# A running merge of three attention groups, wide value matmuls for the new tokens, and other staging buffers in a decoder layer on eight cores

## The chip, the cores and the metric

The kernel runs on all 8 cores of one Trainium2 chip. Each core takes one prompt of 2048 tokens and 4 of the 32 sample tokens (one new token each), and holds all weights for itself; the cores exchange nothing. The time of a run is that of the slowest core, in microseconds (us). Each core has TensorE (PE, matmuls; its weight loads are shown as PEld), VectorE (DVE), ScalarE (ACT), GpSimd (POOL) and SyncE (SP, which here only issues DMAs). Matmuls write to PSUM, which is addressed here as banks of 512 f32 per partition; everything else lies in SBUF or, for long distances, in DRAM scratch.

## What is computed

One decoder layer for the prompt and for the sample tokens. The part that the change touches is the dilated attention: 12 heads of 128 in 3 groups g of 4 heads h, with dilations 1, 4 and 16. A query of a group sees 128 keys of its own residue class modulo the dilation.

```python
for g in range(ATT_GROUPS):                       # 3 groups, 4 heads each
    o, lse, kb, vb = attention(aq[:, :, g], ak[:, :, g], av[:, :, g], dil=(1, 4, 16)[g], 128 keys, bias)
    outs.append(o); lses.append(lse)              # o = P V / den,  lse = max + log(den)
alpha = softmax(stack(lses), axis=0)              # weights of the groups
att_out = sum(alpha * stack(outs), axis=0)        # (tokens, 4 heads * 128)
mixed = sigmoid(gr) * (ret_out @ w_rb) + sigmoid(ga) * (att_out @ w_ab)
x = x + mixed @ w_o
x = x + square(relu(rms_norm(x) @ w_u)) @ w_d
x = x + sigmoid(x @ w_pg) * (ple @ w_pl)
```

Beside it run a retention branch (chunks of 128 tokens, 8 heads), whose output is `ret_out`, and the caches: keys and values of the last 128, 512 and 2048 positions of each group are outputs. For a sample token, the 128 rows of a cache that its query sees, with the new row in place of one, are gathered by stride; scores, softmax over all three groups and values follow.

## The kernel before

**Order of the work.** The Python code records every instruction (an `Op`) with what it reads and writes. `schedule()` (L278) is a planner: a list scheduler with a cost for each instruction, priority by order of recording, and for a DMA a cost of issue (0.55 us on SP) and a latency after its bytes (`DMA_LATENCY`, 2.2 us). `emit()` writes out each engine's instructions in the order that it found, and they wait for each other by semaphores (L397). On the chip this order is fixed: when an instruction waits, everything behind it on its engine waits.

**Stages**, by the times of the profiled execution: norm and transpose of x (0 to 84 us), attention groups 0 and 1 (to about 360 us), group 2 with the values of the sample tokens and the first retention chunks (to 500 us), the other retention chunks (to 733 us), gates and output projection (mix), MLP, and the per-layer embedding at the end (1133 to 1538 us).

**Projections.** L680 is the matmul of `gemm()`: 8 matmuls of 128x512 accumulate one block of a projection. Keys and values of a group are computed with tokens on partitions (`tm_pair`, `tm_full`), copied from PSUM by DVE into one of 5 staging buffers `kvst` (L840), and stored from there to the cache outputs by a DMA (kp, vp); a staging buffer is free again when its store has landed. L847 transposes keys.

**A block of attention.** `scores()`: L903 the matmul, L916 scale and bias (DVE), L919 the negated maximum of each row into `md` (DVE), L922 the exponential with its sum (ACT). `values()`: L933 transposes of P (PE), L937 their copy (DVE), L944 P times V (PE). `core(g, h)` runs 16 tiles of a head, in 4 blocks of 4 tiles, for the groups 0 and 1: L969 copies the unnormalised output from PSUM to `ogs` (DVE), SP stores it to the DRAM scratch `oscr`; negated maxima and denominators go to the scratch `mscr`.

**The merge** is in `core_last(h)`, the third group. For each head the maxima and denominators of groups 0 and 1 are loaded (`ml`), and for each block the outputs of both (`ogl`, 512 KB, in 4 buffers, two of which are named ogx). L1009 to L1021 find the common maximum, the exponentials `ee` of the differences, the denominator and the normalised weights. POOL multiplies the output of group 0 (L1049) and of group 1 in every second block (L1054); ACT does the latter in the other blocks (L1060); POOL adds both (L1063). `finish()` (L1027) takes the product and sum with group 2's own PSUM result, 4 DVE instructions of 128 columns a block; L1035 transposes it (PE), L1038 copies it to `attT` (ACT).

**Sample tokens.** `sample_values(b)` loads, for token b, the 128 value rows of three groups (256 KB each) into `smk` and `smq`, and behind each the one new row into the same buffer. Its inner `rest()` records L1141: for each of 4 heads and 3 groups one f32 matmul with the values as weights and one column of probabilities, 12 in all; L1145 copies the 4 columns. The loads of token h are recorded at head h of group 2, the matmuls at head h+1, the last ones within retention chunk 1.

**Other names.** wr are the 6 weight blocks of the retention (`load_wr`, POOL's queue). `ret_open`, `ret_proj`, `ret_in`, `ret_mix`, `ret_norm` and `ret_sample` are the steps of a retention chunk (L1253 to L1518). `d2d(n)` issues n copies of cache rows, DRAM to DRAM. `ple_in(t)` (L1804) loads a tile of the per-layer embedding through a ring of 4 buffers `pp` and transposes it. L714 is a small f32 matmul for the bias tables at the start.

## Time and profile before

| | us |
|---|---|
| runs, median (three: 1540.83, 1551.37, 1553.70) | 1551.37 |
| profiled execution, its own time | 1539.19 |
| its span, first to last instruction of the slowest core (core 1) | 1538.1 |
| spans of the 8 cores | 1511.6 to 1538.1 |
| mean granted TensorE clock of the 8 cores | 0.965 to 0.971 |

The profile is one execution, on its slowest core. "Busy" is time in which an engine executes; it waits in the rest. The idle time of a group of instructions is what its engine waited just before them, with the engine or DMA that ended the wait. The granted clock is TensorE's: 1.00 is 2.4 GHz, its lower level is 1.2 GHz (0.50). The DMA share is the mean over the core's 16 DMA engines.

### The profile page before, as it was taken

How to read it: one execution, taken by the hardware profiler on the slowest of the kernel's cores; microseconds unless marked ns; L12 is line 12 of the kernel's file. 1: busy time of each engine (PE TensorE's matmuls, PEld its weight loads, DVE VectorE, ACT ScalarE, POOL GpSimd, SP SyncE). 2: the span in 40 equal slices, each digit the busy share in tenths (PEclk: the TensorE clock that was granted, in tenths of full speed). 3: DMA queues.
4: the chain of work that ended last, by engine and by line, in shares of the span. 5: the costliest groups of instructions: out<-in, count | busy, mean ns of one | idle time of the engine just before them, and what ended most of it. 6: DMA issues, size and time to landing. Idle time of an engine off the chain costs nothing.

```text
span 1538.1 us, 25714 instructions; the slowest of 8 cores (1511.6 to 1538.1 us)
## 1 busy us (share of the span) xinstructions
PE 1433.7 (93%) x8657; PEld 771.1 (50%) x8657; DVE 864.5 (56%) x1651; ACT 621.7 (40%) x1354; POOL 259.2 (17%) x287
## 2 busy tenths in 40 slices
PE   4799999897776999997999999999999998999997
PEld 2565555464453445554555554554454444554443
DVE  2654656564554466664434346546656645557776
ACT  2455555444553557675222225431121120220665
POOL 2400000000453454454100001100000000000111
PEclk9899999998886999998999999999999999999999
DMA  9695716788783411108812044799999999730112
GB/s 227 117 153 99 141 53 104 143 199 173 152 200 64 87 39 36 36 26 166 121 28 29 4 89 129 126 140 163 179 157 160 173 161 152 156 69 14 60 79 83
DMA packets 123233, 172.44 MB, mean 112 GB/s; under 512 B 28990, under 2 KB 94583, under 8 KB 122336
## 3 DMA queue, kind: packets, MB, share of 16 engines
q0 software_dynamic: 55200, 43.52, 22.6%
q1 hardware_dynamic: 66368, 83.28, 20.6%
q10 hardware_dynamic: 1536, 43.99, 14.5%
q8 instruction: 72, 1.18, 0.3%
q14 instruction: 57, 0.47, 0.1%
HBM read 184.95 MB, written 75.68 MB: 169 GB/s over the span
## 4 chain that ended last, share of the span: by engine, by line
PE 84%; DMA 6%; issue 3%; ACT 2%; DVE 2%; POOL 1%; SPq 0%; another core or an unknown queue 0%; DVEq 0%; ACTq 0%; POOLq 0%
PE psum L680 74%; PE psum L801 2%; DMA vp<-kvst 1%; DMA kp<-kvst 1%; PE psum L1141 1%; DMA wi<-w_in 1%; PE psum L903 1%; PE psum L933 1%; PE psum L944 1%; DMA xt<-x 1%; ACT pr L922 1%; DMA smq<-vs 1%; PE psum L1447 1%; PE psum L1509 1%; DMA mscr<-md 0%
## 5 line engine op out<-in xcount | busy, mean ns | idle before, releaser
L680 PE MATMUL psum<-wm,rT 128*128 128x512 bf16 (+1 forms) x1088 | 240.1, 379 | 0.0
L680 PE MATMUL psum<-h2T,wm 128*128 128x411 bf16 (+1 forms) x1280 | 227.0, 340 | 0.0
L1801 DVE TENSOR_TENSOR xb<-psum,xb 128x512 f32<-128x512 f32 (+1 forms) x272 | 187.5, 690 | 42.4 <-PE psum L680 31.0
L680 PE MATMUL psum<-wr,hT 128*128 128x512 bf16 x768 | 187.2, 395 | 7.7 <-ACT gs L1300 3.1
L680 PEld LDWEIGHTS psum<-h2T,wm 128*128 128x128 bf16 x1280 | 124.8, 98 | 99.4 <-issue 3.3
L1787 DVE TENSOR_TENSOR rT<-psum,rl 128x411 bf16<-128x411 f32 (+1 forms) x160 | 93.6, 586 | 143.5 <-ACT rl L1785 143.4
L680 PEld LDWEIGHTS psum<-wm,rT 128*128 128x128 bf16 (+1 forms) x1088 | 104.6, 97 | 128.4 <-issue 4.1
L680 PE MATMUL psum<-hT,wi 128*128 128x512 bf16 x640 | 152.5, 384 | 6.5 <-DMA wi<-w_in 3.3
L1785 ACT ACTIVATE rl<-psum 128x411 f32<-128x411 f32 (+1 forms) x160 | 82.1, 513 | 142.5 <-PE psum L680 142.4
L680 PE MATMUL psum<-hT,t1w 128*128 128x411 bf16 (+1 forms) x640 | 120.5, 341 | 4.6 <-ACT sg L1658 4.6
L680 PE MATMUL psum<-wi,hT 128*128 128x512 bf16 (+1 forms) x496 | 118.1, 386 | 3.5 <-DVE kvst L840 3.5
L680 PEld LDWEIGHTS psum<-wr,hT 128*128 128x128 bf16 x768 | 74.0, 101 | 93.0 <-issue 21.8
L922 ACT ACTIVATE pr<-sc,md 128x128 bf16<-128x128 f32 (+1 forms) x192 | 88.6, 461 | 28.3 <-DVE md L919 17.4
L680 PEld LDWEIGHTS psum<-hT,wi 128*128 128x128 bf16 x640 | 61.4, 99 | 69.4 <-issue 11.1
L680 PEld LDWEIGHTS psum<-hT,t1w 128*128 128x128 bf16 x640 | 62.7, 98 | 54.8 <-issue 7.0
L680 PEld LDWEIGHTS psum<-wi,hT 128*128 128x128 bf16 (+1 forms) x496 | 59.0, 126 | 43.8 <-issue 8.0
L1660 DVE TENSOR_TENSOR mm<-psum,sg 128x411 f32<-128x411 f32 (+1 forms) x40 | 23.3, 585 | 99.0 <-PE psum L680 98.9
L1816 ACT COPY pT<-psum 128x256 bf16<-128x256 bf16 (+1 forms) x17 | 5.5, 364 | 181.2 <-PE psum L1812 181.2
L919 DVE TENSOR_REDUCE md<-sc 128x2 f32<-128x512 f32 (+3 forms) x100 | 54.8, 549 | 28.6 <-ACT pr L922 26.6
L1656 ACT ACTIVATE sg<-psum 128x411 f32<-128x411 f32 (+1 forms) x40 | 20.5, 513 | 113.3 <-PE psum L680 86.6
L916 DVE SCALAR_TENSOR_TENSOR sc<-psum,bias 128x512 f32<-128x512 f32 (+2 forms) x100 | 53.2, 549 | 22.9 <-PE psum L903 21.9
L680 PE MATMUL psum<-wm,x2T 128*128 128x512 bf16 (+1 forms) x272 | 61.5, 379 | 0.8 <-ACT x2T L1866 0.8
(202 smaller groups left out, 1973.1 us busy)
## 6 DMA issues: line engine op xcount, KB each, us to landing
ks<-ck ACTq DMA_DIRECT2D x16, 1023.5 KB, 28.1
vs<-cv ACTq DMA_DIRECT2D x16, 1023.5 KB, 24.7
oscr<-ogs SPq DMA_DIRECT2D x32, 256.0 KB, 4.6
wm<-w_up POOLq DMA_DIRECT2D x8, 1024.0 KB, 35.5
wm<-w_dn POOLq DMA_DIRECT2D x8, 1024.0 KB, 49.9
y<-xb SPq DMA_DIRECT2D x16, 512.0 KB, 2.6
kt<-rk SPq DMA_DIRECT2D x17, 432.0 KB, 3.3
xr<-x SPq DMA_DIRECT2D x14, 512.0 KB, 3.9
```

The lines of the kernel that those rows point to most:

```text
L680: ins = e.matmul(out, lhsT=l, rhs=r, start=(i == 0), stop=(i == n - 1))
L801: ins = e.matmul(ps[:, bi, 256 * i:256 * (i + 1)], lhsT=stream_ap(hT[:, k, :], 1, t + i), rhs=wv[:, k, 256 * hp:256 * (hp + 1)], start=(k ...
L903: i = e.matmul(ps[:, sb_, c:c + nk], lhsT=qT[:, 128 * t:128 * (t + 1)], rhs=kT[:, k0:k0 + nk], start=True, stop=True)
L916: dve.op(lambda e, c=c, n=n, nk=nk, sv=sv, bv=bv: e.scalar_tensor_tensor(out=sv, in0=ps[:, sb_, c:c + n * nk].rearrange("p (i k) -> p i k" ...
L919: dve.op(lambda e, i=i, n=n, sv=sv: e.tensor_reduce(out=md[:, 0, i:i + n], in_=sv, axis=AX.X, op=ALU.max, negate=True), reads=[sc_t], writ ...
L922: act.op(lambda e, i=i, c=c, nk=nk: e.activation(out=pr[:, c:c + nk], in_=sc[:, c:c + nk], func=AF.Exp, bias=md[:, 0, i:i + 1], accum_out= ...
L933: i = e.transpose(out=bankbf(pi)[:, c:c + 128], in_=pr[:, c:c + 128], identity=identb)
L1656: act.op(lambda e, s1=s1, b=b, w=w: e.activation(out=s1[:, 0:w], in_=ps[:, b[0], 0:w], func=AF.Sigmoid), reads=[bank_t[b[0]]], writes=[s1_t])
L1660: dve.op(lambda e, s1=s1, m1=m1, b=b, w=w: e.tensor_tensor(out=m1[:, 0:w], in0=ps[:, b[2], 0:w], in1=s1[:, 0:w], op=ALU.mult), reads=[bank ...
L1785: act.op(lambda e, rl=rl, b=b, w=w: e.activation(out=rl[:, 0:w], in_=ps[:, b, 0:w], func=AF.Relu), reads=[bank_t[b]], writes=[rl_t])
L1787: dve.op(lambda e, rl=rl, b=b, w=w, r=r, fi=fi, ts=ts: e.tensor_tensor(out=r[:, fi, ts], in0=ps[:, b, 0:w], in1=rl[:, 0:w], op=ALU.mult), ...
L1801: dve.op(lambda e, b=b, xv=xv, rows=rows: e.tensor_tensor(out=xv, in0=ps[0:rows, b, :], in1=xv, op=ALU.add), reads=[bank_t[b], x1_t[t]], w ...
```

## The change

1. *The merge runs along.* In group 1, each head loads group 0's maxima and denominators, and each block group 0's output (`oga`, a ring of 2). `scores()` takes the smaller of its own negated maximum and that of before (new L929, DVE), so that both are relative to one maximum. A block takes the difference (L998, DVE), its exponential (L1000, ACT), scales the loaded output by it (L1002, POOL) and adds it to its own result in place of the copy (L1006, DVE); at the end of a head the denominators are added (L1017, L1018). Group 2 does the same with the output of group 1 alone, which holds both by now, and multiplies by the reciprocal of the denominator on POOL at the end (L1050), ahead of the transposes (now L1058).

```diff
+    def scores(g, h, ts, Bt, B_t, md, md_t, before=None):
...
+        if before is not None:
+            nm, nm_t = before
+            dve.op(lambda e: e.tensor_tensor(out=md[:, 0, :], in0=md[:, 0, :], in1=nm, op=ALU.min), reads=[md_t, nm_t], writes=[md_t])
...
+            dd, ee = cw[:, 0:16], cw[:, 16:32]
...
+            if g == 1:
+                oa, oa_t, oakey = state["oga"].next()
+                sp.dma(oa.rearrange("p (i c) -> p i c", i=4), oscr[0, h].rearrange("(i p r) c -> r p i c", p=128, r=4)[blk],
+                       oakey, reads=oscr_t[0][h], writes=[oa_t])
...
+                before = None
+                if g == 1:
+                    before = strm(ml[:, 0, :], blk)[:, i:i + 2], ml_t
+                u = scores(g, h, [t, t + 1], Bt, B_t, mdt(t), md_t, before)
...
+                dve.op(lambda e, blk=blk: e.tensor_tensor(out=strm(dd, blk), in0=strm(md[:, 0, :], blk), in1=strm(ml[:, 0, :], blk),
+                                                          op=ALU.subtract), reads=[md_t, ml_t], writes=[cw_t])
+                act.op(lambda e, blk=blk: e.activation(out=strm(ee, blk), in_=strm(dd, blk), func=AF.Exp), reads=[cw_t], writes=[cw_t])
+                a0, a0_t, _ = accring.next()
+                pool.op(lambda e, a0=a0, oa=oa, blk=blk: e.tensor_tensor(
+                    out=a0.rearrange("p (i c) -> p i c", i=4), in0=oa.rearrange("p (i c) -> p i c", i=4),
+                    in1=strm(ee, blk).unsqueeze(2).broadcast_to([128, 4, 128]), op=ALU.mult),
+                    reads=[oa_t, cw_t], writes=[a0_t])
+                dve.op(lambda e, og3=og3, ob=ob, a0=a0: e.tensor_tensor(out=og3, in0=bank(ob), in1=a0, op=ALU.add),
+                       reads=[bank_t[ob], a0_t], writes=[og_t])
...
+            dve.op(lambda e: e.tensor_tensor(out=ee, in0=ee, in1=ml[:, 1, :], op=ALU.mult), reads=[ml_t, cw_t], writes=[cw_t])
+            dve.op(lambda e: e.tensor_tensor(out=md[:, 1, :], in0=md[:, 1, :], in1=ee, op=ALU.add), reads=[md_t, cw_t], writes=[md_t])
```

In `core_last`, the weights of three groups give way to one `ee` and `den`:

```diff
+        dve.op(lambda e: e.tensor_tensor(out=dd, in0=md[:, 0, :], in1=ml[:, 0, :], op=ALU.subtract), reads=[md_t, ml_t], writes=[cw_t])
...
+        dve.op(lambda e: e.tensor_tensor(out=den, in0=ee, in1=ml[:, 1, :], op=ALU.mult), reads=[ml_t, cw_t], writes=[cw_t])
+        dve.op(lambda e: e.tensor_tensor(out=den, in0=den, in1=md[:, 1, :], op=ALU.add), reads=[md_t, cw_t], writes=[cw_t])
...
-                dve.op(lambda e, i=i: e.scalar_tensor_tensor(
-                    out=ak[:, 128 * i:128 * (i + 1)], in0=ps[:, ob, 128 * i:128 * (i + 1)],
-                    scalar=ee[:, 2, 4 * blk + i:4 * blk + i + 1], in1=a0[:, 128 * i:128 * (i + 1)],
-                    op0=ALU.mult, op1=ALU.add), reads=[bank_t[ob], cw_t, a0_t], writes=[ak_t])
+            dve.op(lambda e: e.tensor_tensor(out=a0, in0=bank(ob), in1=a0, op=ALU.add), reads=[bank_t[ob], a0_t], writes=[a0_t])
+            pool.op(lambda e: e.tensor_tensor(
+                out=ak.rearrange("p (i c) -> p i c", i=4), in0=a0.rearrange("p (i c) -> p i c", i=4),
+                in1=den[:, 4 * blk:4 * blk + 4].unsqueeze(2).broadcast_to([128, 4, 128]), op=ALU.mult),
+                reads=[a0_t, cw_t], writes=[ak_t])
```

2. *Values of the sample tokens.* The probabilities of 4 heads are now the weights and the rows of values stream, 512 columns at once; of the result, 4 rows of one bank at partition 32b, the row of head h is wanted only in the columns of head h. ACT copies it to `sov`, and after the fourth token `sample_out()` transposes all and picks the columns. The loads of token 0 are recorded right after the sample softmax; the loads of token h and the matmuls of token h-1 now follow the retention projections of head h, and the last matmuls are in chunk 1 as before. `ret_sample()` moves from chunk 1 to chunk 2.

```diff
+                for g in range(3):
+                    c = 16 * g + 4 * b
+                    ins = e.matmul(ps[32 * b:32 * b + 4, bi, :], lhsT=pT_s[:, c:c + 4], rhs=vts[g][0], start=(g == 0), stop=(g == 2))
                 return ins
...
+            act.op(lambda e: e.copy(out=state["sov"][32 * b:32 * b + 4, :], in_=ps[32 * b:32 * b + 4, bi, :]),
+                   reads=[bank_t[bi]], writes=[state["sov_t"]])
...
+        def tr(e):
+            for h in range(4):
+                ins = e.transpose(out=ps[:, bi, 128 * h:128 * (h + 1)], in_=state["sov"][:, 128 * h:128 * (h + 1)], identity=identf)
+            return ins
...
+        for h in range(4):
+            dve.op(lambda e, h=h: e.tensor_copy(out=attT[:, h, 2048:2052], in_=ps[:, bi, 129 * h:129 * h + 97:32]),
...
-        else:
-            later()
-        later = sample_values(h)
+            later = sample_values(0)
...
+            load_wr(5, marks[2, 0])
             load_wr(4, marks[2, 0])
...
-    load_wr(5, marks[2, 2])
+        if h:
+            later([])
+            later = sample_values(h)
```

3. *Planner.* The latency of a DMA becomes 3.2 us, its issue 0.7 us on SP, and `slack` adds 2.0 us to a load of sample rows and 6.0 us to the one-row load behind it.

```diff
-DMA_LATENCY = 2.2
+DMA_LATENCY = 3.2
...
-                    o.t1 = now + DMA_LATENCY
+                    o.t1 = now + DMA_LATENCY + o.slack
...
+        sp.dma(v, cache[b, 0:W:DILS[g], :], key, writes=t, after=state["x_in"], slack=2.0)
+        sp.dma(v[0:1, :], new[b, W - 1:W, :], key, reads=[new_t], writes=t, slack=6.0)
```

4. *Buffers.* `kvst` has 6 in place of 5, `sc` 3 in place of 4, `md` 4 in place of 2; `ogl` becomes four of 512 columns, and the `acc` ring gets the two `oga` buffers in group 2. The lower part of the region shrinks, and the last `load_wr` moves ahead, since its space is free earlier.

```diff
-        state["kv"], o = ringbuf("kvst", o, 512, F32, 5)
-        state["ac1"], o = ringbuf("ac1", o, 512, F32, 2)
+        state["kv"], o = ringbuf("kvst", o, 512, F32, 6)
+        state["oga"], o = ringbuf("oga", o, 512, F32, 2)
...
+            items.extend(ringbuf("ogx%d_" % i, OQ + 8192 * i + 4096, 512, F32, 2)[0].items)
+        accring.items.extend(state["oga"].items)
+        state["ogl"] = Ring(items[::2] + items[1::2])
```

5. *Later stages.* Five steps of the mix stage issue two `d2d` copies each. `ple_load(t)` is split from `ple_in(t)`, and `ple_in` runs one MLP step later.

```diff
+        if 1 <= f <= 5:
+            d2d(2)
...
+        if 2 <= j <= 7:
+            for t in range(3 * (j - 2), min(3 * (j - 1), 17)):
+                ple_in(t)
         if 1 <= j <= 6:
             for t in range(3 * (j - 1), min(3 * j, 17)):
-                ple_in(t)
+                ple_load(t)
```

**In the order of the instructions.** The first excerpt is from PE, at the last blocks of group 1's last head: L903 scores, L933 transposes of P (`pr`), L944 P times V (`vf`, `pT`), L847 transposes of keys. Before:

```order
L903 MATMUL psum<-qk_98 128x128
L903 MATMUL psum<-qk_98 128x256
L933 MATMUL psum<-identb,pr_77 128x128 x3
L944 MATMUL psum<-vf_100,pT_83 128x128 x3
L933 MATMUL psum<-identb,pr_78 128x128 x4
L944 MATMUL psum<-vf_100,pT_84 128x128 x4
L933 MATMUL psum<-identb,pr_79 128x128 x3
L944 MATMUL psum<-vf_100,pT_85 128x128 x3
L933 MATMUL psum<-identb,pr_80 128x128 x4
L944 MATMUL psum<-vf_100,pT_83 128x128 x4
L847 MATMUL psum<-identb,kb_112 128x128 x4
L847 MATMUL psum<-identb,kb_113 128x128 x4
```

Now, with L682 a projection (one row for 8 matmuls), L942 the transposes of P and L953 P times V:

```order
L682 MATMUL psum<-wi_51,hT 128x512 x8
L942 MATMUL psum<-identb,pr_76 128x128 x3
L682 MATMUL psum<-wi_50,hT 128x512 x8
L953 MATMUL psum<-vf_101,pT_82 128x128 x3
L682 MATMUL psum<-wi_51,hT 128x512 x8
L942 MATMUL psum<-identb,pr_77 128x128 x4
L953 MATMUL psum<-vf_101,pT_83 128x128 x4
L682 MATMUL psum<-wi_51,hT 128x512 x8
L942 MATMUL psum<-identb,pr_78 128x128 x3
L953 MATMUL psum<-vf_101,pT_84 128x128 x3
L942 MATMUL psum<-identb,pr_79 128x128 x4
L953 MATMUL psum<-vf_101,pT_82 128x128 x4
```

Four projections of the next group now stand in and around these four pairs of transposes and values (a fifth pair begins with the row above these); the last two pairs have none in them.

The second excerpt is also from PE, in group 2, where the matmuls for the values of a sample token (now L1155) stand. Before, the third token's 12 (L1141, the first of them is the last row here) came behind this:

```order
L944 MATMUL psum<-vf_101,pT_85 128x128 x4
L933 MATMUL psum<-identb,pr_79 128x128 x4
L680 MATMUL psum<-wr_124,hT 128x512 x8
L903 MATMUL psum<-kT_99,qk_98 128x128 x4
L680 MATMUL psum<-wr_125,hT 128x512 x8
L1035 MATMUL psum<-identb,atk_119 128x128 x4
L944 MATMUL psum<-vf_101,pT_83 128x128 x4
L944 MATMUL psum<-vf_101,pT_84 128x128 x4
L933 MATMUL psum<-identb,pr_80 128x128 x4
L1035 MATMUL psum<-identb,atk_120 128x128 x4
L903 MATMUL psum<-kT_99,qk_98 128x128 x8
L1141 MATMUL psum<-sm,smk_115 128x1
```

Now the rows from the second token's matmuls on are these (L1058 transposes of the merged block, L1340 and L1446 of the retention):

```order
L1155 MATMUL psum<-smk_118,sm 4x512
L1058 MATMUL psum<-identb,atk_120 128x128 x4
L942 MATMUL psum<-identb,pr_80 128x128 x4
L682 MATMUL psum<-wr_138,hT 128x512 x8
L1058 MATMUL psum<-identb,atk_121 128x128 x4
L953 MATMUL psum<-vf_102,pT_83 128x128 x4
L1340 MATMUL psum<-identb,qkr_135 128x128 x8
L942 MATMUL psum<-identb,pr_81 128x128 x4
L682 MATMUL psum<-wr_140,hT 128x512 x8
```

and on to the third token's:

```order
L953 MATMUL psum<-vf_102,pT_84 128x128 x4
L942 MATMUL psum<-identb,pr_76 128x128 x4
L682 MATMUL psum<-wr_140,hT 128x512 x8
L942 MATMUL psum<-identb,pr_77 128x128 x4
L1446 MATMUL psum<-qkT_128 128x128 x8
L953 MATMUL psum<-vf_102,pT_82 128x128 x4
L682 MATMUL psum<-wr_127,hT 128x512 x8
L1058 MATMUL psum<-identb,atk_119 128x128 x4
L953 MATMUL psum<-vf_102,pT_83 128x128 x4
L1155 MATMUL psum<-smk_116,sm 4x512
L1155 MATMUL psum<-smk_117,sm 4x512
```

Between the two there are four projections and thirteen shorter pieces; between the first and the second token's, not shown, there are seven and thirteen.

The third excerpt is from DVE, in group 1, near the end of the last head. Before, the output of a block is copied (L969) between scores (L916, L919) and the copy of P (L937):

```order
L969 COPY ogs_103<-psum 128x512
L1091 TENSOR_REDUCE sm<-smq_114 128x4
L919 TENSOR_REDUCE md_86<-sc_74 128x2
L1093 SCALAR_TENSOR_TENSOR sm<-sm 128x16
L916 SCALAR_TENSOR_TENSOR sc_75<-psum,bias_71 128x128
L937 COPY pT_84<-psum 128x384
L919 TENSOR_REDUCE md_86<-sc_75 128x1
L916 SCALAR_TENSOR_TENSOR sc_75<-psum,bias_71 128x256
```

Now the sum L1006 stands there, with `acc` from POOL, and the minima L929 and the difference L998 around it (L922 scale and bias, L925 the maximum, L946 the copy of P):

```order
L1006 TENSOR_TENSOR ogs_103<-psum,acc_94 128x512
L925 TENSOR_REDUCE md_87<-sc_73 128x2
L922 SCALAR_TENSOR_TENSOR sc_75<-psum,bias_71 128x512
L946 COPY pT_84<-psum 128x384
L929 TENSOR_TENSOR md_87<-md_87,ml_89 128x2
L998 TENSOR_TENSOR cw_92<-md_87,ml_89 128x4
L925 TENSOR_REDUCE md_87<-sc_74 128x1
L922 SCALAR_TENSOR_TENSOR sc_74<-psum,bias_71 128x256
L925 TENSOR_REDUCE md_87<-sc_74 128x1
L929 TENSOR_TENSOR md_87<-md_87,ml_89 128x2
L946 COPY pT_82<-psum 128x512
```

The sum has the next scores and the next copy of P behind it, and three small instructions have come in.

## Rows read from the trace of the kernel before

**Rows 1.** Busy time, share and instructions of each engine, from the page.

```profile
PE 1433.7 (93%) x8657; PEld 771.1 (50%) x8657; DVE 864.5 (56%) x1651; ACT 621.7 (40%) x1354; POOL 259.2 (17%) x287
```

**Rows 2.** Stretches: us, busy (count) of PE, PEld, DVE, ACT, POOL; PEclk, DMA share, GB/s.

```profile
84.00:269.00 185.00, 184.85 (x1238) 108.81 (x1236) 104.99 (x209) 101.51 (x276) 3.54 (x4) 1.00 0.60 110
269.00:345.00 76.00, 69.70 (x404) 41.26 (x404) 47.29 (x99) 33.84 (x88) 0.00 (x0) 0.98 0.80 168
345.00:400.00 55.00, 40.55 (x250) 22.92 (x250) 24.47 (x52) 32.37 (x109) 7.78 (x9) 0.88 0.91 174
400.00:450.00 50.00, 42.02 (x281) 28.92 (x281) 31.22 (x85) 23.85 (x81) 30.16 (x27) 0.81 0.67 157
450.00:500.00 50.00, 34.41 (x219) 20.11 (x217) 25.27 (x86) 22.95 (x51) 19.43 (x17) 0.67 0.44 110
```

**Rows 3.** The same view, of shorter stretches.

```profile
350.00:360.00 10.00, 6.08 (x33) 3.51 (x34) 4.20 (x8) 4.66 (x12) 0.00 (x0) 0.52 0.63 184
398.00:408.00 10.00, 9.54 (x42) 7.21 (x43) 0.72 (x3) 1.61 (x6) 3.20 (x3) 0.53 0.34 93
442.00:452.00 10.00, 8.94 (x40) 7.10 (x41) 3.50 (x11) 2.33 (x9) 5.35 (x5) 0.51 0.62 126
...
473.00:490.00 17.00, 9.96 (x44) 4.69 (x44) 7.91 (x23) 5.85 (x12) 11.54 (x11) 0.52 0.41 63
```

**Rows 4.** PE's groups, 200:500: instruction, count, busy, mean ns, idle before, releasers.

```profile
L680 PE MATMUL psum<-wi,hT 128*128 128x512 bf16 x288 | 70.2, 390 | 3.5 <-DVE kvst L840 3.5
...
L1141 PE MATMUL psum<-sm,smk 128*128 128x1 f32 x64 | 13.4, 313 | 12.0 <-ACT pr L922 6.0 <-DMA smq<-vs 5.6 <-ACT attT L1038 0.4
...
L1035 PE MATMUL psum<-identb,atk 128*128 128x128 bf16 x64 | 7.2, 243 | 6.2 <-DVE atk L1027 4.5 <-ACT attT L1038 1.6 <-ACT cw L1014 0.2
```

**Rows 5.** Chain that ended last, two stretches: start us, us, what.

```profile
266.27 18.00 DMA kp<-kvst
...
398.46 5.25 PE psum L1141 x24
...
409.98 1.73 PE psum L680 x8
...
422.12 2.72 PE psum L1141 x24
...
425.30 6.82 DMA smk<-cv
...
433.44 9.28 DMA smq<-vs
...
443.06 5.25 PE psum L1141 x24
...
491.67 4.23 PE psum L1141 x24
```

**Rows 6.** Timeline of PE near the start: start, us, instruction, what released it.

```profile
7.57 1.43 PE L714 MATMUL psum<-ohg,rbx 33*4 33x383 f32 x2 [7.57 <-DMA ohg<-ohg]
```

**Rows 7.** DMA issues: queue, count, KB each, median us from issue to landing.

```profile
ogl<-oscr SPq DMA_DIRECT2D x8, 512.0 KB, 7.2
...
pp<-pp POOLq DMA_DIRECT2D x16, 64.0 KB, 56.9
```

**Rows 8.** Groups by form, as in 4, of DVE (200:500) and POOL (200:510).

```profile
L1027 DVE SCALAR_TENSOR_TENSOR atk<-psum,cw,acc 128x128 bf16<-128x128 f32 x64 | 20.5, 346 | 3.0 <-POOL acc L1063 0.6 <-DVE atk L1027 0.2
...
L969 DVE COPY ogs<-psum 128x512 f32<-128x512 f32 x18 | 12.4, 691 | 9.0 <-PE psum L944 4.0 <-PE psum L903 2.9 <-PE psum L977 1.6
...
L1011 DVE TENSOR_TENSOR cw<-cw,ml 128x32 f32<-128x32 f32 x4 | 1.8, 458 | 0.2
...
L1015 DVE TENSOR_TENSOR cw<-cw,ml 128x32 f32<-128x32 f32 x4 | 0.8, 188 | 0.7 <-ACT cw L1014 0.7
...
L1063 POOL TENSOR_TENSOR acc<-acc,ac 128x512 f32<-128x512 f32 x16 | 20.0, 1265 | 2.3 <-ACT ac L1060 2.1
L1049 POOL TENSOR_TENSOR acc<-ogx,cw 128x512 f32<-128x512 f32 x8 | 8.3, 1040 | 7.3 <-DVE atk L1027 6.8 <-DVE cw L1018 0.4
```

163 lines of the change are left out of this document (74 added, 89 removed).

## The prediction

> **What bounds the kernel now.** I read the page's table of engines first: TensorE (PE) is busy 93% of the span [rows 1]. Then the stretches [rows 2]: from 84 to 269 us PE is busy 184.85 of 185 us, so nothing done there on another engine can gain. From 269 to 500 us it is busy 69.70, 40.55, 42.02 and 34.41 of 76, 55, 50 and 50 us: 6.3 + 14.4 + 8.0 + 15.6 = 44.3 us idle. This is the end of attention group 1, all of group 2, and the new tokens' values, and it is where the change works. No engine is full there: VectorE (DVE) has 25.27 of the last 50 us. So the loss is latency between engines in a fixed order, not throughput.
>
> The idle time has a second price. In four stretches of this region the granted clock is 0.51 to 0.53, the lower level (1.2 GHz), each behind or among waits of PE [rows 3]. PE is busy 6.08 + 9.54 + 8.94 + 9.96 = 34.5 us in them; at 2.4 GHz about half of it would do, 17 us less. The pool to win from is thus 44 + 17 us, 4% of the time.
>
> Who makes PE wait: values of the new tokens (L1141) 12.0 us, the transposes of the merged output (L1035) 6.2 us, projections behind a staging copy (L680 wi,hT, released by kvst L840) 3.5 us [rows 4]. The rest are gaps of about 1 us where the order holds nothing but links of one chain.
>
> **The change, part by part.**
> *Waits ahead of the sample values.* A bulk load lands, then a one-row load into the same buffer is issued; that 2 KB row took 9.28 us from issue to landing, although it is tiny [rows 5]. The planner had counted 2.2 us, and now counts 3.2 plus 6.0 for such a row. The chain of loads, 425.3 to 442.7 us in the trace, is 17 us. In the new order PE has seven projections and thirteen short pieces between the first and second group of value matmuls, and four and thirteen between the second and third (second excerpt of the order). At 1.73 us a projection [rows 5] and about 0.25 us a piece that is 15.5 and 10 us. So the first, second and last group should find their rows there within 2 us, and the third may lack up to 7, of which waits for the merge in between use some: 12.0 becomes 5. **-7** (bounds -12 and 0).
>
> *The matmuls themselves.* 48 with one column each, f32, took 5.25, 2.72, 5.25 and 4.23 us, 17.45 together [rows 5]; the 2.72 is at full clock. They become 12 with 512 columns, plus four f32 transposes. The trace has no such shape. Nearest is the f32 matmul of 383 columns (L714): 1.43 us for its two records [rows 6]. For 512 columns that is 1.91 us, or 0.96 if that row ran at the lower level, which it does not show. Twelve cost 11.5 or 22.9 us; L714 ran just after PE's first wait, as those stretches of half clock do, so I lean to the lower price and take 13.5. **-4** (bounds -6 and +6). A gain only by clock: at full level the old 48 would be 4 x 2.72 = 10.9 us.
>
> *Tail of group 1.* Of the 14.4 us idle in 345:400, 6 belong to the value wait at 398 us; the other 8 are the alternation of L933, L944 and L847 that the first excerpt of the order shows, about nine gaps. Afterwards four projections stand inside it, and two of the five pairs are still bare. **-3** (bounds -6 and 0).
>
> *Staging buffers 5 to 6.* The waits are DMAs of 256 KB that take up to 18.00 us to land [rows 5]; one more buffer gives one more copy of cover, but not more bandwidth. **-2** (bounds -3.5 and 0).
>
> *Merge in group 2.* Per head, DVE loses 16 instructions of 346 ns (L1027) for 4 of 512 columns, about 691 ns as L969 [rows 8]: 22.1 us less 11.1 over four heads. Of the small instructions nine leave and eight come: nothing. GpSimd (POOL) per block loses an add of 1265 ns and half a product of 1040 and gains one product [rows 8], ScalarE its 32 scalings. Against it, the merged block now passes through one more engine before its transpose: after the DVE sum a POOL product of 1.04 us and a hop. Per block 4 x 0.346 = 1.4 us on DVE become 0.69 + 1.04 + about 0.15. The path is half a microsecond longer, but the planner knows it and puts other work between; DVE, which everything else waits for, is freed by 11 us of the 81 it is busy from 345 to 500 us [rows 2]. The load of the sixth retention weight also moves ahead, since its space is free earlier. Of 15.6 us idle in 450:500 I take **-5** (bounds -10 and +6).
>
> *Merge in group 1.* New: 32 minima and 16 differences on DVE, near 0.18 us each (L1015), 8.6 us; 16 POOL products, 16 tiny exponentials, 16 loads of 256 KB, 8 of 8 KB. The DVE copy L969 becomes a sum of the same width. DVE is busy 47.29 of 76 us, so 8.6 us over 140 fit under PE. What can cost: the sum waits for POOL, POOL for the load; the third excerpt shows that behind it on DVE stand the next scores and the copy of P, for which PE waits. The loads add about as much to the queues as group 2 loses, since there half of each pair load goes. Cover is the ring of two: 16 blocks between 215 and 355 us, 8.7 us each, so a load is issued one to two blocks ahead, against a median of 7.2 us for the double-sized load of before [rows 7]. **+3** (bounds 0 and +45, the slower rival below).
>
> *Clock.* Idle would go from 44.3 to 44.3 - 7 - 3 - 2 - 5 + 3 = 30, a third less; the 17 us of half-clock loss shrink alike. **-6** (bounds -12 and 0).
>
> *Per-layer embedding and cache copies.* Its transposes are recorded a stage later and its loads with them. With four buffers a load still waits for the transpose before it, so each is issued one stage of about 58 us ahead of its use, as before, and takes 56.9 us to land [rows 7]; the waits for it stay. **0** (bounds -9 and +2). Ten cache copies move into the stage at 733 us; its weights are loaded three steps ahead: 0.
>
> Sum: -7 - 4 - 3 - 2 - 5 + 3 - 6 = -24. The profiled execution took 1539.19 us (span 1538.1 and 1.1 around it), so 1515. The three runs and it average 1546.3, 7 us above it, which I add: **1522 us**. The median of the runs is 1551.37; all bounds of "same" are against that.
>
> One rule of the Trainium skill speaks against the merge. First the row: L1011, a DVE product of two SBUF operands, 32 columns, has a mean of 458 ns over four, while the like L1015 has 188 [rows 8], and POOL's products run beside both. The Trainium skill (SBUF — State Buffer, Who interferes with whom) says that a VectorE instruction with two SBUF inputs and a GpSimd one that reads SBUF exclude each other, the later one blocking fully. By that rule, the trace agrees; the price is in a rival below.
>
> **Rivals.**
> 1. *Slower: the running merge stalls DVE in group 1.* Place: the sum behind each block's POOL product. For it: a landing of 18.00 us at 266 us and a DMA share of 0.80 behind it [rows 2, 5]. Against it: POOL has nothing else in 269:345 (0.00 us). If 12 blocks wait 4 us each, +48; the other terms but the clock give -21, and the clock is lost in place of won, +6: 1546 + 48 - 21 + 6 = 1579. It decides from about 2.5 us a block.
> 2. *Nothing measurable.* The value waits go (-8) but the longer path to the transposes takes back the merge's 5, the tail gaps only move, and with them the half clock: -7 - 2 is left, 1537 or more.
> 3. *Port conflict.* 48 minima and 24 further small ones in group 1 have two SBUF inputs. Worst: each blocked for a whole product of 1.04 us, 72 x 1.04 = 75 us of DVE, a third of it on the path: +25, 1547. Likely: 0.27 us (458 less 188) for the 16 minima of group 2, +2 on the path, which the forecast survives.
> 4. *Larger gain.* The order closes nearly all: -12 - 6 - 5 - 3 - 9 and -12 by clock, -47, on 1546: 1499.
>
> **How the numbers follow.** Chances: forecast (1507 to 1534) 0.50, larger gain 0.15, nothing 0.17, port conflict 0.05, slower 0.13. The range must leave out no more than 2 in 10: from 1497, below which I put 0.08, to 1552, above which lie rival 1 nearly whole. About 1% is what a measurement of this kernel can tell: faster by over 1% is below 1536: 0.69. Slower by over 1% is above 1567: 0.08, the worse half of rival 1. Within: 0.23.
>
> **What the changed profile would show.** Right: idle before the value matmuls (new L1155) at 4 us or less and their busy time 11 to 15 us; granted clock over 0.9 from 345 to 500 us but for short pieces; the stage after 500 us of unchanged length. The merge is right if PE's idle time before the transposes (new L1058) is under 6 us and DVE's idle time on POOL in group 1 is small. Wrong: DVE idle before new L1006, released by POOL, of over 2 us a block; PE waits for P or scores in 205:345, where there are few now; value matmuls near 1.9 us each at full clock; or new minima (L929) with a mean far above 180 ns.

## The result and the profile after

The changed kernel's median is 1537.03 us of 18 runs (lowest 1530.29), that of the kernel before 1548.68 us in the same comparison; the ratio is 0.9927 with a 95% interval of 0.9899 to 0.9954, a gain of 0.7% or about 11 us. Forecast were 1522 us, a gain of 29 us on the median of 1551.37 (24 us by the sum of the terms). The measured time lies in the range given, but the change is well under half of the forecast one, and within the 1% that was called "same". In some runs the cores of one die have a lower granted clock and the time is some per cent longer; the ratios and intervals below leave those runs out.

The profiled run of the changed kernel took 1541.02 us; its slowest core is 6, with a span of 1539.7 us (about 1% of its matmul records are missing). Its table of engines, against [rows 1]:

```profile
PE 1418.5 (92%) x8478; PEld 751.5 (49%) x8589; DVE 867.5 (56%) x1655; ACT 619.5 (40%) x1342; POOL 263.8 (17%) x296
```

Stretches as in [rows 2], same columns (us; busy of PE, PEld, DVE, ACT, POOL; granted clock; DMA share; GB/s):

```profile
84.00:269.00 185.00, 181.11 (x1191) 106.30 (x1209) 104.69 (x231) 99.51 (x275) 10.93 (x11) 1.00 0.64 113
269.00:345.00 76.00, 65.87 (x382) 38.54 (x388) 43.06 (x104) 36.68 (x95) 7.33 (x7) 0.93 0.77 168
345.00:400.00 55.00, 40.70 (x230) 22.38 (x234) 26.06 (x57) 23.99 (x71) 6.21 (x7) 0.87 0.78 149
400.00:450.00 50.00, 37.69 (x230) 18.78 (x236) 27.42 (x61) 26.29 (x89) 20.39 (x20) 0.87 0.93 169
450.00:500.00 50.00, 35.72 (x245) 17.21 (x247) 24.54 (x61) 23.89 (x58) 19.96 (x19) 0.86 0.42 110
```

In 84:269, which was full before, PE has 3.9 us of idle time; 2.3 of them lie behind 200 us, where group 1 begins, and some of the rest is missing records. PE's idle time in 269:345 is 10.1 us where it was 6.3, in the three stretches behind it 14.3, 12.3 and 14.3 where it was 14.4, 8.0 and 15.6. The clock is better: 0.87 and 0.86 in the last two, where it was 0.81 and 0.67. Who makes PE wait, by groups of shape from 200 to 520 us (count | busy us, mean ns | idle time before, and what ended it), against [rows 4]. These rows, and all below for which no core is named, are of the slowest core:

```profile
L682 PE MATMUL psum<-wi,hT 128*128 128x512 bf16 x278 | 72.1, 406 | 7.1 <-DVE sc L922 3.6 <-DVE kvst L846 3.1
...
L942 PE MATMUL psum<-identb,pr 128*128 128x128 bf16 x183 | 19.0, 224 | 10.6 <-ACT pr L931 10.1 <-DVE pT L946 0.5
L953 PE MATMUL psum<-vf,pT 128*128 128x128 bf16 x176 | 18.6, 229 | 8.8 <-DVE acc L1049 3.8 <-DVE pT L946 2.7 <-DVE md L929 2.3
L1155 PE MATMUL psum<-smk,sm 128*4 128x512 f32 x24 | 13.2, 696 | 0.1
...
L1058 PE MATMUL psum<-identb,atk 128*128 128x128 bf16 x64 | 6.4, 225 | 1.8 <-ACT attT L1061 1.8
...
L1121 PE MATMUL psum<-cf_sb,sm 128*16 128x128 f32 x3 | 0.8, 403 | 4.9 <-DVE sm L1110 4.9
```

The waits ahead of the value matmuls (L1155) are gone, 0.1 us for 12.0 (that was the slowest core; the eight cores had 4.0 to 12.0, 8.3 in the mean), and those ahead of the transposes of the merged output (L1058) are 1.8 for 6.2. In their place stand 10.6 us before the transposes of P, 8.8 us before P times V, and 4.9 us before the transposes of the sample scores (L1121). Before, these three were:

```profile
L933 PE MATMUL psum<-identb,pr 128*128 128x128 bf16 x183 | 19.7, 230 | 3.6 <-ACT pr L922 3.5
L944 PE MATMUL psum<-vf,pT 128*128 128x128 bf16 x176 | 18.5, 231 | 2.9 <-DVE pT L937 2.9
...
L1104 PE MATMUL psum<-cf_sb,sm 128*16 128x128 f32 x3 | 0.5, 273 | 0.0
```

**A table by stages.** Clock times drift between kernels, so I cut each trace at instructions instead: the last output copy of group 0 and of group 1 (L969 before, L995 and L1006 after), the last copy of `attT` in group 2 (L1038), the last transposes of the retention (L1509), the last product of the mix stage (L1664), and the first sigmoid of the last stage (L1876). Each number is a mean over the 8 cores of the profiled execution, in us. "Idle" is the time of the two attention stages in which PE has no matmul. "Half clock" is, over the whole run, half of PE's busy time at granted clock 0.5, that is, what the lower level cost. The ratio is that of the timed runs to the kernel before on the same chip.

| kernel | ratio, 95% interval | group 1 | group 2 | retention | MLP | idle, groups 1 and 2 | half clock |
|---|---|---|---|---|---|---|---|
| before | 1 | 146.4 | 132.0 | 242.6 | 515.2 | 39.6 | 36.2 |
| changed | 0.993, 0.990 to 0.995 | 155.2 | 129.2 | 238.3 | 512.0 | 47.5 | 22.2 |
| e8 changed, again | (one run) | 152.2 | 128.7 | 237.5 | 509.9 | 46.6 | 17.9 |
| e1 without running merge | 0.981, 0.975 to 0.986 | 145.9 | 119.0 | 238.2 | 507.9 | 34.2 | 16.1 |
| e2 without the minima | 0.977, 0.968 to 0.986 | 147.5 | 112.7 | 241.7 | 507.9 | 31.3 | 18.7 |
| e3 before, new planner numbers | 0.989, 0.983 to 0.996 | 144.9 | 123.1 | 241.1 | 508.6 | 33.6 | 27.8 |
| e4 no slack for key rows | 0.992, 0.989 to 0.994 | 154.9 | 126.2 | 241.9 | 508.1 | 42.8 | 21.8 |
| e5 finer bookkeeping of md | 0.974, 0.971 to 0.977 | 139.7 | 111.3 | 244.2 | 510.9 | 28.6 | 13.5 |
| e7 e1 with old planner numbers | 0.990, 0.987 to 0.994 | 153.3 | 121.7 | 242.2 | 514.0 | 42.3 | 24.7 |
| e9 before, finer bookkeeping | 0.999, 0.996 to 1.001 | 146.4 | 132.1 | 241.7 | 517.4 | 36.2 | 38.4 |
| e10 narrow value matmuls | 0.997, 0.995 to 1.000 | 153.4 | 137.5 | 236.1 | 511.2 | 45.8 | 30.3 |
| e11 before, buffers only | 0.998, 0.995 to 1.001 | 150.4 | 135.4 | 237.1 | 517.9 | 38.9 | 39.2 |
| e12 e5 and e4 | 0.972, 0.968 to 0.976 | 139.1 | 107.4 | 242.8 | 509.9 | 25.1 | 12.3 |
| e13 e12 without the minima | 0.970, 0.964 to 0.976 | 144.1 | 104.4 | 246.1 | 511.7 | 24.6 | 16.7 |
| e14 e12 without running merge | 0.978, 0.973 to 0.984 | 142.6 | 119.4 | 238.5 | 513.2 | 32.2 | 19.5 |
| e15 e12 again | 0.972, 0.968 to 0.977 | 139.4 | 107.8 | 243.3 | 512.1 | 25.0 | 13.1 |

Between two profiles of the same kernel (changed and e8, e12 and e15) a stage of attention differs by up to 3 us, so I read differences above that. The MLP stage differs by more from chip to chip (e4, which does the same work there as the changed kernel, has 508.1 us), so I don't read differences of 4 us in it. e6 has no row; e14, the same kernel but for the slack, gives the stages.

e8 is the changed kernel once more, beside the experiments on another chip:

> The changed kernel once more, for its stages on the same chip as the runs beside it. Both theories: group 1 at 153 to 157 us, group 2 at 127 to 131, waits of VectorE on the exponentials of 25 us or more; if group 1 is under 150, the comparison of stages between chips doesn't hold.

Measured: one run of 1521.86 us, group 1 at 152.2 us, a little under the 153 to 157 expected, group 2 at 128.7 us, and 28.0 us of VectorE's waits on the exponentials in the mean of the cores. Stages of attention can be compared between chips to 3 us. The ratios are less sure: this one run is 0.988 of the median of the kernel before on its chip (1541.04), under the interval of the changed kernel, 0.990 to 0.995, which was measured on another. Where e5, e10 and e12, measured on that chip, are read against 0.993 below, 0.988 may be the right number there: the gains of e5 and e12 over the changed kernel would then be 0.5% smaller, the loss of e10 0.5% larger.

The rows of before and of the changed kernel hold the riddle: the change gave back 14 us of half clock and added 8 us of idle time, 5 in group 1 (10.8 to 16.0) and 3 in group 2 (29.1 to 31.8), where the prediction's terms take 14 us away.

### The profile page after: what moved, and what is told of

The parts are those of the page before. It is cut to its first block, busy times and chain, and to the rows that moved or that the text cites. A ratio compares the mean times of both kernels' runs of the same rounds, so it can differ in the third digit from the quotient of the medians.

```text
span 1539.7 us, 25506 instructions; the slowest of 8 cores (1506.4 to 1539.7 us)
## 1 busy us (share of the span) xinstructions
PE 1418.5 (92%) x8478; PEld 751.5 (49%) x8589; DVE 867.5 (56%) x1655; ACT 619.5 (40%) x1342; POOL 263.8 (17%) x296
## 3 DMA queue, kind: packets, MB, share of 16 engines
q10 hardware_dynamic: 1536, 43.99, 13.5%
## 4 chain that ended last, share of the span: by engine, by line
PE 83%; DMA 5%; issue 4%; ACT 3%; DVE 3%; POOL 1%; another core or an unknown queue 1%; SPq 0%; DVEq 0%; ACTq 0%; POOLq 0%
PE psum L682 74%; DMA wi<-w_in 2%; PE psum L807 1%; DMA smk<-qscr 1%; DMA vp<-kvst 1%; PE psum L953 1%; PE psum L1155 1%; ACT pr L931 1%; PE psum L942 1%; PE psum L909 1%; DMA sts<-S_s 1%; ACT raw L1531 1%; DMA ohs<-ohs 0%; PE psum L1784 0%
## 5 line engine op out<-in xcount | busy, mean ns | idle before, releaser
L682 PE MATMUL psum<-wm,rT 128*128 128x512 bf16 (+1 forms) x1063 | 236.9, 379 | 1.3
L682 PE MATMUL psum<-h2T,wm 128*128 128x411 bf16 (+1 forms) x1280 | 225.6, 338 | 0.7 <-DVE rT L1822 0.7
L682 PE MATMUL psum<-wr,hT 128*128 128x512 bf16 x739 | 178.1, 389 | 15.0 <-DVE sm L1520 5.9
L682 PEld LDWEIGHTS psum<-h2T,wm 128*128 128x128 bf16 x1280 | 124.4, 98 | 99.0 <-issue 2.5
L682 PEld LDWEIGHTS psum<-wm,rT 128*128 128x128 bf16 (+1 forms) x1088 | 104.7, 97 | 128.5 <-issue 3.6
L682 PE MATMUL psum<-hT,wi 128*128 128x512 bf16 x614 | 149.6, 387 | 15.0 <-DMA wi<-w_in 8.1
L682 PE MATMUL psum<-wi,hT 128*128 128x512 bf16 (+1 forms) x482 | 119.8, 394 | 7.3 <-DVE sc L922 3.6
L682 PE MATMUL psum<-hT,t1w 128*128 128x411 bf16 (+1 forms) x640 | 118.7, 337 | 1.6 <-ACT sg L1689 1.0
L682 PEld LDWEIGHTS psum<-wr,hT 128*128 128x128 bf16 x768 | 72.9, 99 | 96.4 <-issue 22.6
L682 PEld LDWEIGHTS psum<-hT,wi 128*128 128x128 bf16 x640 | 61.7, 99 | 77.4 <-issue 19.3
L682 PEld LDWEIGHTS psum<-hT,t1w 128*128 128x128 bf16 x640 | 61.9, 97 | 50.3 <-issue 1.9
L682 PEld LDWEIGHTS psum<-wi,hT 128*128 128x128 bf16 (+1 forms) x496 | 59.5, 127 | 47.7 <-issue 13.3
L925 DVE TENSOR_REDUCE md<-sc 128x2 f32<-128x512 f32 (+3 forms) x100 | 55.0, 550 | 44.1 <-ACT pr L931 40.6
L922 DVE SCALAR_TENSOR_TENSOR sc<-psum,bias 128x512 f32<-128x512 f32 (+2 forms) x100 | 54.2, 550 | 23.9 <-PE psum L909 22.3
L682 PE MATMUL psum<-wm,x2T 128*128 128x512 bf16 (+1 forms) x268 | 61.3, 379 | 1.7 <-ACT x2T L1910 1.4
## 6 DMA issues: line engine op xcount, KB each, us to landing
y<-xb SPq DMA_DIRECT2D x16, 512.0 KB, 2.6
xr<-x SPq DMA_DIRECT2D x14, 512.0 KB, 4.1
```

Of the source, the lines that this page charges most:

```text
L682: ins = e.matmul(out, lhsT=l, rhs=r, start=(i == 0), stop=(i == n - 1))
L922: dve.op(lambda e, c=c, n=n, nk=nk, sv=sv, bv=bv: e.scalar_tensor_tensor(out=sv, in0=ps[:, sb_, c:c + n * nk].rearrange("p (i k) -> p i k" ...
L925: dve.op(lambda e, i=i, n=n, sv=sv: e.tensor_reduce(out=md[:, 0, i:i + n], in_=sv, axis=AX.X, op=ALU.max, negate=True), reads=[sc_t], writ ...
```

## Experiments on the running merge

**e1: all of the change but the merge.** The functions `core` and `core_last` are those of before, on the changed kernel's buffers (`sc` 3, `kvst` 6, `md` 4):

```diff
-                u = scores(g, h, [t, t + 1], Bt, B_t, mdt(t), md_t, before)
+                u = scores(g, h, [t, t + 1], Bt, B_t, mdt(t), md_t)
...
-            load_wr(5, marks[2, 0])
...
+    load_wr(5, marks[2, 2])
```

> The changed kernel with the merge of before put back (all three groups merged in the third, four columns blocks of 128 on VectorE, sixth retention weight loaded after group 2); planner numbers, wide value matmuls, the later recording, the 6 staging buffers and the later stages stay as changed. Theory A (the running merge lost in group 1 what the rest of the change won): group 1, from the last output copy of group 0 to that of group 1, falls from a mean of 155.2 us over the cores to about 147 (before: 146.4), group 2 grows by 3 to 5 us, and the whole is 4 to 6 us shorter than the changed kernel, near 0.989 of before. Theory B (group 1 is longer because of the planner's new numbers): group 1 stays at 153 to 156 us, and without the merge's gain in group 2 the whole is 0.993 to 1.0 of before.

Measured: 0.981, group 1 145.9 us, group 2 119.0. Theory A holds for group 1. But group 2, which by theory A would grow, is 10 us shorter without the merge. So the merge as built costs 1.2% (0.993 against 0.981), or 18 us, 9 us in group 1 and 10 in group 2. The two ratios are from different chips; e4 (0.992), which is as fast as the changed kernel, ran on the same chip as e1, so the difference stands. All the rest of the change gives 1.9%, about 29 us.

**e2: the minima left out.** Each group keeps its own maximum; the weights of the groups are then wrong, and that is the part of the computation that this kernel changes.

```diff
-        if before is not None:
+        if False:
```

> The changed kernel without the 48 minima between maximum and exponential (new L929): each group keeps its own maximum, so its weights are wrong, all other instructions stay. Theory A1 (what group 1 lost is the longer chain scores, maximum, minimum, exponential, transposes): PE's wait for the exponentials before the transposes of P falls from 10.6 us (200 to 520 us) to about 5, group 1 from 155.2 to 151 or less, the whole by 4 us or more. Theory A2 (it is the sum behind GpSimd's product and the loads): group 1 stays within 1.5 us of 155.2, the whole within 3 us of the changed kernel.

Measured: 0.977; group 1 147.5 us, group 2 112.7. PE's wait for the exponentials before the transposes of P fell from 10.1 to 7.4 us only, less than theory A1 said, but its times are met. The loads of 256 KB, GpSimd's products and the sums are all still there, so theory A2 falls. 48 instructions of 0.18 us on VectorE, 8.6 us in all, cost 1.5% of the time (0.993 against 0.977, whose interval is a wide one), about 23 us: 7.7 in group 1 and 16.5 in group 2, less 3 given back in the retention. The new wait before the transposes of the sample scores (L1121) goes too: in the mean of the cores it is 4.5 us in the changed kernel, 0.5 without the minima and 0.0 in e1. A price of more than twice the instructions' own time calls for something that they make wait. The groups of VectorE show it, all shapes together, 200 to 500 us before and 200 to 520 us after:

```profile
L919 DVE TENSOR_REDUCE md<-sc 128x1 f32<-128x256 f32 (+3 forms) x64 | 32.9, 516 | 19.2 <-ACT pr L922 17.7 <-DVE sc L916 0.2
```

```profile
L925 DVE TENSOR_REDUCE md<-sc 128x2 f32<-128x512 f32 (+3 forms) x65 | 33.7, 519 | 33.1 <-ACT pr L931 30.1 <-DVE cw L998 0.5
...
L929 DVE TENSOR_TENSOR md<-md,ml 128x2 f32<-128x2 f32 (+1 forms) x48 | 8.6, 179 | 1.7 <-DVE md L925 0.8
```

VectorE sits idle before the maxima for 30.1 us until an exponential of ScalarE has ended, 17.7 before; without the minima (e2) it is 14.5. A maximum needs no exponential. The timeline of VectorE in group 2 of the changed kernel (start, length, instruction, [idle before <- what ended it]):

```profile
439.62 0.69 DVE L925 TENSOR_REDUCE md<-sc 128x4 f32<-128x512 f32 x1 [5.23 <-ACT pr L931]
440.41 0.16 DVE L929 TENSOR_TENSOR md<-md,ml 128x4 f32<-128x4 f32 x1
...
443.78 0.69 DVE L925 TENSOR_REDUCE md<-sc 128x4 f32<-128x512 f32 x1 [1.87 <-ACT pr L931]
444.57 0.16 DVE L929 TENSOR_TENSOR md<-md,ml 128x4 f32<-128x4 f32 x1
```

and of ScalarE, which starts with the first exponential after that minimum:

```profile
440.67 0.40 ACT L931 ACTIVATE pr<-sc,md 128x128 bf16<-128x128 f32 x1 [1.15 <-DVE md L929]
...
441.73 0.40 ACT L931 ACTIVATE pr<-sc,md 128x128 bf16<-128x128 f32 x1
...
442.59 0.41 ACT L931 ACTIVATE pr<-sc,md 128x128 bf16<-128x128 f32 x1
...
443.19 0.40 ACT L931 ACTIVATE pr<-sc,md 128x128 bf16<-128x128 f32 x1
443.50 0.19 ACT L931 ACTIVATION_READ_ACCUMULATOR pr<-sc,md 128x1 f32 x1
```

The maximum of a block ends, the minimum follows it 0.1 us later and lasts 0.16, the first exponential starts 0.1 us after that, the fourth of the block begins at 443.19, and only after it has ended (with its sum, at 443.69) does VectorE take the next block's maximum, at 443.78. Two engines take turns, and the minimum stands inside each turn. The cause is in the bookkeeping: the buffer `md` of a head holds maxima in columns 0 to 15 and sums in 16 to 31, and is one name. An exponential reads its maximum from `md` and writes its sum there, the next maximum writes to `md`, and so it waits for the last exponential, though they touch different columns. I call this a false dependence.

**e5: names for parts of md.** The same instructions, the same buffer; only what counts as a conflict is told finer.

```diff
-    mdring, o = ringbuf("md", o, 32, F32, 4)
+    for i in range(4):
+        md_.append((view("md%d" % i, o, 32, F32), P.tiles(["mx%d_%d" % (i, j) for j in range(8)] + ["su%d_%d" % (i, j) for j in range(8)], o, 128), "md%d" % i))
...
-                   reads=[sc_t, md_t], writes=[pr_t, md_t])
+                   reads=[sc_t, md_t[0]], writes=[pr_t, md_t[1]])
```

> The changed kernel with finer bookkeeping of the buffer md alone: maxima and sums of each pair or block of tiles are told apart, so the maximum of the next block (L925) no longer waits for the exponentials of the block before, whose sums go to other columns of the same buffer. No instruction is added or removed. Theory D (the minima cost so much because VectorE and ScalarE take turns: maximum, minimum, exponentials, next maximum; VectorE's idle time before the maxima, released by the exponentials, is 29 us in the changed kernel, 13 before and 14 without the minima): that idle time falls under 3 us, group 1 goes from 155 to 150 or less, group 2 from 129 to 121 or less, the whole to 0.980 of before or less. Rival E (it is only the length of one chain, 0.2 us and a hop more per block, and the other order that the planner makes of it): group 1 and 2 together gain under 4 us, the whole stays at 0.990 or more.

Measured: 0.974, group 1 139.7, group 2 111.3. (The expectation's "13 before" is e1's 13.0; the kernel before has 17.7.) The maxima's wait for exponentials is gone, and PE waits 3.9 us for exponentials before the transposes of P (L946) where it waited 10.1:

```profile
L929 DVE TENSOR_REDUCE md<-sc 128x1 f32<-128x256 f32 (+3 forms) x64 | 32.1, 513 | 1.2
...
L933 DVE TENSOR_TENSOR md<-md,ml 128x2 f32<-128x2 f32 (+1 forms) x48 | 9.3, 201 | 1.3 <-DVE md L929 0.2
```

```profile
L946 PE MATMUL psum<-identb,pr 128*128 128x128 bf16 x192 | 19.9, 225 | 4.6 <-ACT pr L935 3.9 <-DVE cw L1047 0.8
```

Theory D holds, and by more than it asked for: 1.9% against the changed kernel (1.3% against e8's one run), with the same instructions. Their order is another, though, since the planner sees the same dependences as the chip: the run shows what the false dependence costs, not how much of it is waiting on the chip and how much the order that the planner made around it. Rival E (only one chain's length) allowed 4 us; groups 1 and 2 together gained 33 (30 against e8), of which the retention gave back 6.

**e6, e9, e13: where the turns cost, and where not.** The same bookkeeping in the kernel without the running merge (e6), in the kernel before (e9), and with it but without the minima (e13, whose weights of the groups are wrong again).

> The kernel of the run without the running merge (0.981 of before), with the same finer bookkeeping of md. By theory D the turns cost less here, since no minimum stands in them (9 us of VectorE's idle time before the maxima): 2 to 6 us are gained, 0.977 to 0.980. If the turns cost by themselves and not through the minimum, the gain is as large as in the kernel with the running merge.

> The kernel before with the finer bookkeeping of md alone (as in the run on the changed kernel, 0.974 of before). By theory D the turns cost little where no minimum stands between maximum and exponential: VectorE's idle time before the maxima is about 19 us there, PE waits for exponentials 3.5 us, so group 1 and 2 gain 2 to 7 us together, 0.995 to 0.998 of before. If the false dependence is the main loss in both kernels: 0.990 or less, and then the running merge has nothing to do with it.

> The kernel with finer bookkeeping of md and slack on value rows only (0.972 of before), now without the 48 minima (each group keeps its own maximum, so its weights are wrong). If the minima cost only through the turns of VectorE and ScalarE: within 3 us of the kernel with them, where the difference was 23 us (0.977 against 0.992) with the coarse bookkeeping. If the 0.2 us and a hop in each block's chain cost by themselves: 6 us or more shorter, 0.968 or less.

Measured: e6 0.976 (0.973 to 0.980) against e1's 0.981, a gain of 0.4% by the middle of the ratios, which the intervals don't separate. e9 0.9985 (0.996 to 1.001): nothing, though VectorE's wait before the maxima went from 19.2 us to 1.0:

```profile
L923 DVE TENSOR_REDUCE md<-sc 128x1 f32<-128x128 f32 (+3 forms) x64 | 31.4, 510 | 1.0
```

e9 came out just above its forecast of 0.995 to 0.998. So the false dependence is old and was harmless: 19 us of idle VectorE cost nothing that can be measured. PE's waits only moved: in the mean of the cores those ahead of the value matmuls went from 8.3 to 1.3 us and those ahead of P times V from 2.9 to 6.6. With the minimum in each turn the same dependence decides. e13 at 0.970 against e12's 0.972 and e15's 0.972 says that with the finer names nothing measurable is left of the minima's price: 0.2% between the middles, with intervals of 0.5% to either side, where it was 1.5%; the three stages from group 1 to the retention are even 4 us longer without them.

**e14 and e15: what the merge is worth by itself.** e12's kernel once more, and the same without the running merge, with more runs of each.

> The kernel without the running merge, with the finer bookkeeping of md and slack on value rows only. By the terms of the prediction (-5 in group 2, +3 in group 1) the kernel with the merge is 2 us shorter with its part of the clock 4 to 6: this one at 0.975 to 0.977, group 2 about 10 us longer (121 against 111) and group 1 the same, which then is given back in part by longer retention stages (244 against 239) with the merge. If the merge gives nothing: 0.971 to 0.973.

> The kernel with finer bookkeeping of md and slack on value rows only, again, in five rounds for the comparison with the one without the merge: 0.970 to 0.974 of before, group 1 at 139 us, group 2 at 107 to 111, retention at 243.

Measured: 0.978 (0.973 to 0.984) without and 0.972 (0.968 to 0.977) with it, and before that 0.976 (e6) and 0.974 (e5) with the other slack. Both pairs point the same way, 0.2 and 0.6%, and the intervals overlap. The stages say where: group 1 142.6 without and 139.4 with it, group 2 119.4 and 107.8, retention 238.5 and 243.3; in sum 10 us shorter with the merge. The prediction gave it 5 us in group 2 less 3 in group 1, with a share of the clock; here it is 12 in group 2 and 3 more in group 1, less 5 in the retention. The merge is most likely a gain once the turns are gone; its size stays uncertain between 0 and 1%.

## Experiments on the planner's numbers, the value matmuls and the buffers

**e3: only the planner's new numbers, on the kernel before.**

```diff
-DMA_LATENCY = 2.2
+DMA_LATENCY = 3.2
...
-        o.us = 0.9 if self.name == "pool" else 0.55
+        o.us = 0.9 if self.name == "pool" else 0.7
```

and slack 2.0 and 6.0 on the rows of the sample tokens.

> The kernel before with only the planner's new numbers (latency 3.2, issue 0.7, slack 2.0 and 6.0 for the rows of the sample tokens). If the numbers alone remove the waits ahead of the value matmuls: PE's idle time before them falls from 12.0 us to 5 or less, the granted clock behind them is up, group 2 is 8 to 12 us shorter than 132.0, the whole 0.992 to 0.995 of before. If the numbers only shift the waits (the rows of keys, which are spaced out as well): idle time appears before the transposes of the sample scores (L1104), 3 to 5 us, and the whole is 0.997 to 1.003. Group 1 stays at 146 us by theory A, and goes to 150 or more by theory B.

Measured: 0.989 (0.983 to 0.996), group 2 123.1 for 132.0. The first forecast holds. No instruction differs from before, only the order, and PE's wait ahead of the value matmuls went from 12.0 us (8.3 in the mean of the cores) to nothing (core 0, 200:520):

```profile
L1143 PE MATMUL psum<-sm,smk 128*128 128x1 f32 x64 | 12.6, 300 | 0.0
...
L1106 PE MATMUL psum<-cf_sb,sm 128*16 128x128 f32 x3 | 0.5, 272 | 0.0
```

There is no new wait before the transposes of the sample scores (L1106) either, and group 1 stays at 144.9, so theory B falls. But other waits grew: in the mean of the cores those ahead of the transposes of P, of P times V and of the transposes of the merged output are 20.3 us together, where they were 12.5. So that the gain comes from the value waits is not shown; what the table shows is 6 us less idle time in groups 1 and 2, 8 us less half clock, and 7 us less in the MLP, where no rows of the sample tokens are loaded (of these 7 a part may be the chip). By the middles of the ratios, these numbers alone are worth more than the whole change (1.1 against 0.7%).

**e7: e1 with the old numbers.**

> The kernel without the running merge, and without the planner's new numbers: what is left of the change are the wide value matmuls, the later recording, the staging buffers and the later stages. If these add up with the numbers (0.989 alone) to the 0.981 of both: 0.991 to 0.993 of before, with the matmuls for the values busy for 13 us and PE waiting 8 us or more before them. If the later recording alone already covers the transfers: under 3 us of wait before them and 0.984 or less. If the new numbers are needed for anything else to gain: 0.997 or more.

Measured: 0.990 (0.987 to 0.994), where e1 with the new numbers has 0.981. The time is as forecast, the wait is not: PE waits 1.4 us before the value matmuls in the mean of the cores, not 8 or more, so the rest of the change covers most of the transfers without the new numbers. So the numbers are worth about 1% on both kernels, and the wide matmuls, the later recording, the buffers and the late stages together another 1%. They add up: 1 + 1 less the 1.2 of the merge is 0.8, near the 0.7 of the change. Group 1 is 7 us longer with the old numbers on these buffers (153.3 against 145.9), where on the kernel before they made 1.5. A part of that is PE's wait behind the staging copies, 4.0 us in the mean of the cores against e1's 0.8; no run tells the rest.

**e4 and e12: slack on value rows only.** The key rows of the sample tokens lose theirs.

```diff
-            sample_rows(kbuf, ck[g], ks[g], g, b, ksn_t[g])
+            sample_rows(kbuf, ck[g], ks[g], g, b, ksn_t[g], (0.0, 0.0))
```

> The changed kernel, with the planner's slack for sample rows on the value rows only, not on the key rows. Theory C (the new wait of 4.9 us of PE at the transposes of the sample scores, L1121, comes from key rows that the slack spaces out): that wait falls under 1.5 us, group 2 is 4 to 6 us shorter with its half clock, the whole 3 to 6 us shorter than the changed kernel. Rival: the wait is that of a transfer which lands late wherever it stands; then it stays over 3 us and the whole is the same within 2 us.

> The changed kernel with finer bookkeeping of md (0.974 of before) and with the planner's slack on value rows only. In that kernel PE still waits 4.75 us ahead of the transposes of the sample scores. If the key rows' slack is behind this wait: it goes, and the whole is 0.971. If the two are as independent of each other as in the changed kernel, where the slack made no difference that was measured (0.9915 against 0.9927): 0.973 to 0.975.

Measured: e4 0.992 (0.989 to 0.994), as the changed kernel; PE's wait at L1121 is 4.1 us on its slowest core, 4.9 in the changed kernel. Theory C falls for this kernel. In e12 (0.972) that wait, now L1125, is 1.6 us:

```profile
L1125 PE MATMUL psum<-cf_sb,sm 128*16 128x128 f32 x3 | 0.5, 270 | 1.6 <-ACT qk L878 1.6
```

e12 and e15 are at 0.972 where e5 was at 0.974, not separated by the intervals; group 2 is 4 us shorter in both. In the changed kernel the wait comes with the minima and not with the slack, since e1 and e2 keep the slack and have 0.0 and 0.5 us of it. The link between the two is not shown: the trace names the load of the query row behind an earlier buffer (smk<-qscr, 5.0 us of VectorE's idle time before L1105, 0.0 in e1 and e2), and no run moved that load alone. e12 is the best kernel of the study, 2.8% below the kernel before; its fastest run took 1496.99 us.

**e10: the value matmuls narrow again**, at their new places.

```diff
-                    ins = e.matmul(ps[32 * b:32 * b + 4, bi, :], lhsT=pT_s[:, c:c + 4], rhs=vts[g][0], start=(g == 0), stop=(g == 2))
+                        ins = e.matmul(ps[:, bi, h:h + 1], lhsT=vts[g][0][:, 128 * h:128 * (h + 1)], rhs=pT_s[:, c:c + 1],
```

> The changed kernel with the matmuls for the sample values as before (48 with one column each, VectorE's copy of 4 columns, no transposes at the end), at the new places in the order. The prediction gave the wide form 4 us, as a gain by the clock. In the trace of the changed kernel six records of the wide form take 2.73 us at the upper clock, the 24 of the old form 2.72 us. Theory F (nothing but the clock tells them apart, and the waits are what brings it down): the narrow form takes 11 to 14 us too, the whole is within 3 us of the changed kernel. Rival G (the narrow form itself lowers the clock): granted clock 0.5 behind each group again, 17 us busy and 5 us or more added.

Measured: 0.997 (0.995 to 1.000) against 0.993 (0.990 to 0.995): 0.4%, or 6 us, between the middles, on different chips, with intervals that just touch; against e8's one run on e10's own chip it is 14 us. Theory F falls and rival G is the nearer: group 2 is 8 us longer (137.5 against 129.2), with 20.7 us of half clock in it against 10.6, though the matmuls are busy for 15.6 us and not 17. Neither form has a wait ahead of it (0.1 us). At the upper clock both take the same, 24 records in 2.79 us and 6 records in 2.74; but in e10 the four groups took 15.6 us in the mean of the cores (12.0 in the changed kernel), and the half clock of the run is 30.3 us against 18 to 22. PE's timeline of e10, core 7:

```profile
422.82 3.52 PE L1156 MATMUL psum<-sm,smk 128*128 128x1 f32 x24
...
450.35 5.22 PE L1156 MATMUL psum<-sm,smk 128*128 128x1 f32 x24
...
481.01 3.68 PE L1156 MATMUL psum<-sm,smk 128*128 128x1 f32 x24
...
506.97 2.79 PE L1156 MATMUL psum<-sm,smk 128*128 128x1 f32 x24
```

and stretches right behind or over three of those groups:

```profile
425.00:431.00 6.00, 6.00 (x29) 3.79 (x29) 1.28 (x4) 2.51 (x9) 0.00 (x0) 0.50 1.11 177
446.00:458.00 12.00, 10.47 (x64) 9.15 (x65) 6.18 (x14) 7.57 (x25) 4.92 (x5) 0.50 0.33 93
483.00:489.00 6.00, 6.00 (x28) 4.00 (x29) 1.82 (x9) 2.16 (x4) 0.60 (x1) 0.50 0.41 131
```

From 425 to 431 us PE is busy all of the time, and the granted clock is 0.50. The same core of e8, the changed kernel, behind the first three wide groups, of which the first is shown:

```profile
414.98 2.74 PE L1155 MATMUL psum<-smk,sm 128*4 128x512 f32 x6
```

```profile
418.00:424.00 6.00, 4.26 (x29) 2.15 (x27) 1.42 (x4) 4.28 (x14) 0.00 (x0) 1.00 1.08 247
443.00:455.00 12.00, 7.99 (x60) 4.16 (x57) 3.38 (x10) 10.86 (x28) 0.00 (x0) 1.00 0.41 126
470.00:476.00 6.00, 5.31 (x50) 2.82 (x49) 3.79 (x15) 4.42 (x8) 0.00 (x0) 1.00 0.43 132
```

Here PE is busy for 4.26 of 6 us, and has full clock. In the prediction the half clock hung on idle time alone; by these stretches it also hangs on what PE is busy with. The fourth group of e10, at 506.97, ran at the upper level all through. The order around the groups differs a little too, since the planner costs the two forms differently, so I don't put the 6 us wholly on the matmuls.

**e11: 6 staging and 3 score buffers, on the kernel before.**

```diff
-    sring, o = ringbuf("sc", o, 512, F32, 4)
+    sring, o = ringbuf("sc", o, 512, F32, 3)
...
-        state["kv"], o = ringbuf("kvst", o, 512, F32, 5)
+        state["kv"], o = ringbuf("kvst", o, 512, F32, 6)
```

> The kernel before with 6 staging buffers in place of 5 and 3 score buffers in place of 4, nothing else. If the staging copies gain what was predicted: PE's idle time before the projections, released by the copies kvst, falls from 3.5 to 1.5 us, the whole 1 to 3 us shorter. If the score buffer that is taken away costs more: PE waits before scores (L903) and transposes of P rise by 3 us or more in group 1 and 2, the whole 0.998 to 1.005 of before.

Measured: 0.998 (0.995 to 1.001). The wait behind the staging copies did not fall: it is 3.6 us in the mean of the cores and was 2.5 before (0.2 to 5.9 from core to core; the 3.5 is the slowest one's). Groups 1 and 2 are 4 and 3 us longer and the retention 5 us shorter. The buffers are worth nothing that can be measured, and the expected gain by the staging copies is not there.

## Why the prediction was off, step by step

*What bounds the kernel*, and that 44 us of idle time and 17 us of half clock are the pool, held: e12 took 15 us of idle time (39.6 to 25.1 in the two groups) and 24 us of half clock (36.2 to 12.3) out of it.

*Waits ahead of the sample values, -7.* 12.0 us went to 0.1, more than the 7, but the 12.0 was the slowest core's; in the mean of the cores it was 8.3 us to 0.0, so the size came out near by luck. The 4.9 us that came up before L1121 belong to the merge's bill, since they are not there in e1 and e2. e3 shows the numbers to be worth about 1%, 16 us, where this step and its clock gave 10 us; up to 7 of the 16 are in the MLP, for which the prediction had 0, and e7 shows that the rest of the change removes most of the waits by itself. The size is about right, the way to it is not shown.

*Matmuls, -4.* I had 17.45 to 13.5 us; the profile of core 6 has 13.2, the mean of the cores 16.1 to 12.0. At the upper clock one wide matmul takes 0.91 us, so the lower of the two prices (0.96) was the right one. The reason was right too: the two forms take 2.7 us a group at the upper clock, and the gain is in how often they run there. The Trainium skill (FP8 and Floating Point Precision, TensorE Precision Notes) gives true FP32 four passes through the array; the trace agrees, 0.91 us for an f32 matmul of 512 columns against 0.22 us for a bf16 one (1.73 us for 8).

*Tail of group 1 and staging, -3 and -2.* Neither shows. PE is idle for 14.3 us in 345:400 where it was 14.4, and the wait behind staging copies is 3.5 us in the mean of the cores where it was 2.5. e11 has nothing from the buffers alone.

*Merge in group 2, -5.* Its two halves came true (L1058 waits 1.8 us, and the sums take VectorE 11 us, 11 less than the old four instructions a block), and the step still failed: group 2 is 10 us longer with the merge than without it (e1), and e2 puts all of that, and 6 us more, on the minima. The step priced the path behind the merge and said of the small instructions "nine leave and eight come: nothing". Four of those eight are the minima of a head, one in each block; the nine that leave stood once, at the end of a head's scores. An exchange of equal counts moved four of them in front of the exponentials. (Of the 48 minima 32 are in group 1 and 16 in group 2; rival 3 puts all 48 in group 1.)

*Merge in group 1, +3.* With the step before, this is the one that failed: the two together gave -2 us, and the runs have +18 (e1). "8.6 us over 140 fit under PE" is a statement on VectorE's load; the minimum stands between the maximum and the exponential, in a ring that closes through `md`: maximum, minimum, exponentials, next maximum. In each of 48 turns it adds 0.16 us and a hop of 0.1, 12.5 us in the ring by the timeline above. In group 1 that is 8.3 us for 32 turns, where e2 measured 7.7; in group 2 it is 4.2 us for 16 turns, where e2 measured 16.5. The other 12 us of group 2 are not explained by the length of the turns. That the planner, whose order follows the same dependences, moved PE's work behind them is likely, and no run shows it by itself. Cost of the minima: 23 us (e2), 29 with all that the false dependence took (e5: 0.993 to 0.974). The waits to be seen if the step was wrong were named, "PE waits for P or scores in 205:345", and that is where they stand: group 1 has 5 us more of idle time and is 9 us longer.

*Clock, -6.* It was -14 in the profile (36.2 to 22.2), nearly half of it in the retention stages (9.2 to 2.6), which the prediction held unchanged. It came without less idle time, which was to bring it. The sign named for the clock, over 0.9 from 345 to 500 us, did not come: the rows have 0.86 and 0.87.

*Later stages, 0.* MLP 515.2 to 512.0 and 509.9 (e8), inside the bounds of -9 and +2; e3, with the planner's numbers alone and no other loads, has 508.6, so the new places of the loads need not be what brings it.

*The rivals.* Rival 1 (the sum behind GpSimd's product): VectorE waits 1.0 us for it in group 1, so this fell:

```profile
L1006 DVE TENSOR_TENSOR ogs<-psum,acc 128x512 f32<-128x512 f32 x16 | 11.0, 689 | 6.0 <-PE psum L953 2.7 <-PE psum L942 1.2 <-POOL acc L1002 1.0
```

Rival 2 (nothing measurable, 1537 or more; its text has -8 for the value waits and its sum -7) met the number, by another way than it gave: it looked for the loss in the path to the transposes, and it was in front of P. Rival 3 (the shared port) exists and is small. The minima by their line, with the shortest, median and longest in ns:

```profile
L929 DVE TENSOR_TENSOR md<-md,ml x48: 141/153/752, 212.4 to 471.6; 128x2 f32<-128x2 f32 x32, 128x4 f32<-128x4 f32 x16
```

```profile
412.32 0.22 DVE L929 TENSOR_TENSOR md<-md,ml 128x4 f32<-128x4 f32 x1
...
417.00 0.57 DVE L929 TENSOR_TENSOR md<-md,ml 128x4 f32<-128x4 f32 x1
...
428.34 0.75 DVE L929 TENSOR_TENSOR md<-md,ml 128x4 f32<-128x4 f32 x1
```

```profile
411.48 2.04 POOL L1071 TENSOR_TENSOR acc<-ogx,cw 128x512 f32<-128x512 f32 x2 [24.52 <-DVE sm L1140]
...
415.52 2.04 POOL L1071 TENSOR_TENSOR oga<-ogx,cw 128x512 f32<-128x512 f32 x2
...
427.04 2.04 POOL L1050 TENSOR_TENSOR atk<-acc,cw 128x512 bf16<-128x512 f32 x2
```

The three long ones start while GpSimd runs a product, and end within 0.05 us of that product's end (412.54, 417.57 and 429.09; the rows show pairs of products of 1.02 us each). All 48 together take 8.6 us where 48 of the median would take 7.3. That is 1.3 us, and the 75 us of the worst case were far off. By the rule of the Trainium skill (SBUF — State Buffer, Who interferes with whom) that the prediction weighed, this is what is to be expected; it decides nothing here. Rival 4 (1499 us) did not happen; only with `md` told apart, which the change does not do, does the kernel come near it (medians 1503.12 us in e5, 1497.70 in e12).

## What to carry to other kernels

A small instruction is priced by the ring of dependences that it enters, not by its engine's load: follow the chain until it closes, through every buffer that two engines write, and multiply by the turns. Where an engine waits for one whose result it doesn't use, the bookkeeping is too coarse; that can be free (e9) and cost 2% once an instruction is added to the ring (e5). And a wait that goes from one place can come back at another (e3, e9): compare the idle time of whole stages. Last, before a structural change is judged, run the tables that set the order alone: here the planner's numbers alone (0.989) were worth as much as all the rest of the change without the merge (e7, 0.990).

## What the runs showed of the hardware

PE busy without a gap ran at granted clock 0.50, from 425 to 431 us of e10, behind 24 records of f32 matmuls with one column each; the same region with 6 records of 512 columns kept 1.00 with PE busy 71% of the time (e8, 418 to 424 us). One column f32 with 128x128 weights and 512 columns f32 with 4 columns of weights cost the same at the upper level, 2.79 and 2.74 us for one token's 12 and 3 matmuls.
